# Opening of an attention layer: queries of the first head pair projected ahead of the second half of its keys

## The chip, the cores and the metric

One core of one Trainium2 chip. The metric is device microseconds (us) of one execution of the whole program. The engines are TensorE (PE, with its weight loads as PEld), VectorE (DVE), ScalarE (ACT), GpSimd (POOL) and SyncE (SP, which issues most DMAs). Each runs its own list of instructions in order and waits on semaphores for the others.

## What is computed

A decoder trunk of two layers over 1024 tokens of 1024 features. Layer 0 is a gated short convolution with a SwiGLU feed-forward network (FFN). Layer 1 is the attention this case is about, again with an FFN. Its core, cut from the reference:

```python
xn = _rms_norm(x, g[0])
shared = _shared_kv(x, kv_norm_g, kv_w)          # k, v = split(_rms_norm(h, g_kv) @ w_kv)
q = (x @ w_q).reshape(b, s, N_HEADS, HEAD_DIM) * (HEAD_DIM ** -0.5)
for (window, dil), (k_cat, v_cat) in zip(DILATED_GROUPS, shared):   # (128,1),(512,4),(2048,16)
    sc = einsum(q, k_cat) + bias                 # bias = -slope * distance, masked to the band
    p = exp(sc - max); den = sum(p); o = (p / den) @ v_cat
out = sum over the three, weighted by their softmax denominators
mix = out @ w_o
```

There are 16 heads of 64 features, worked in 8 pairs.

## The kernel before, in words

Products are done in about float32 accuracy: each operand is split into a high part (rounded to the matmul's type, by a CAST on ACT) and a low part (the rest, by a subtraction on DVE), and three products of 8 matmuls are summed (high by high, low by high, high by low). So a projection of 512 tokens for one head pair is 24 matmuls of 128x512 in one of two PSUM banks.

The **opening** stands between the last FFN product of layer 0 and the first attention step. In it the normalized tokens of the second half, tiles 4 to 7, are turned (transposed) by PE one by one, each by eight small matmuls out of `acc_tile`; ACT then makes `x_hi` (L1622) and DVE `x_lo` (L2252). Between these turns PE runs six projections for head pair 0 (`project_first`, L1538). They are named here K0, K1 (keys of tokens 0 to 511 and 512 to 1023), V0, V1 and Q0, Q1. The order is the table `OPENING`, of (part, half) with part 0 keys, 1 values, 2 queries. `TURNS` gives the matmul count ahead of which each of the four turns stands. A half-1 projection needs `x_lo` of all eight tiles.

The projection weights come as *chunks*: chunks 0, 1, 2 are the keys', values' and queries' weights of pair 0, chunks 3, 4, 5 those of pair 1. SP loads a chunk (`load_projection`) into one of two raw buffers, POOL multiplies it by the norm's gains (`scale_chunk`, L3426), and `prepare` makes its high part on ACT (L1611) and its low part on DVE (L2241). The split weights lie in three buffers: chunks 0 and 3 share `w_second_100`, 1 and 4 `w_second_98`, 2 and 5 `w_second_99`. So ACT's `prepare` of chunk 3 waits on `chunk_done`, which counts chunks whose half 1 is done:

```python
act.wait_ge(chunk_done.sem, moving + (min(n - SPLIT_RING + 1, chunk0["oproj"]) + CREDIT))
```

For chunk 3 that is one chunk of attention, the keys: K1 must have run. For chunk 4 it is V1.

A finished projection is taken by `project` on ACT (high part, L2088 keys, L2099 queries) and DVE (low part, L3012 keys, L3017 queries); values are turned by PE and split (L2105 ACT, L3027 DVE). The parts of keys and queries are then copied by DMAs on SP's queue into `k_stack` (all 1024 keys, four DMAs of 512 KB) and `q_stack` (four DMAs per half). The first scores matmul (L1555) waits for the stacked keys and for the first half of the stacked queries; `q_parts` holds one half at a time.

DVE also makes the **bias tables** in the opening: `distances` (L2985), `window_counts(0)` (L2970), `window_counts(1)` (L2973 to L2980, four operations), `window_counts(2)` (three), `masked_logs`, `log_of(2)`, `log_of(3)`, and `head_bias` (L3035, two operations). The bias is needed by DVE's first operation of an attention step, which adds it to the scores and finds the row's minimum (L3060). After that comes ACT's exponential (L2193), whose function table is loaded by an `ACT_TABLE_LOAD` ahead of it.

Of the kernel before, what the change touches and what calls it, by code (L numbers as in the profile page):

```python
# [21 lines left out]
F32 = mybir.dt.float32  # L22
# [8 lines left out]
HALF = 512  # L31
# [129 lines left out]
def trunk(nc, x, norm_g, conv_in_w, conv_w, conv_out_w, kv_norm_g, kv_w, q_w, o_w,  # L161
# [25 lines left out]
    with ExitStack() as ctx:  # L187
# [18 lines left out]
        rden = keep("rden", [2])  # L206
        neg_half = keep("neg_half", [1])


# [498 lines left out]

        OPENING = ((0, 0), (1, 0), (0, 1), (2, 0), (1, 1), (2, 1))
        TURNS = {22: HT, 36: HT + 1, 46: HT + 2, 48: HT + 3}  # L710

# [14 lines left out]
        def _(sp):  # L726
# [221 lines left out]
            def stack_first():  # L948
                for e in range(2):
                    sp.wait_ge(*k_lo_done.at("attn", 2))  # L950
                    for b in range(2):
                        sp.dma_start(att["k_stack"][b * HD:(b + 1) * HD, e].bitcast(F32),
                                     att["k_parts"][e * HD:(e + 1) * HD].bitcast(F32)).then_inc(k_stacked[e], 16)
                load_projection(5, 0)
                for h in range(2):
                    sp.wait_ge(*q_lo_done.at("attn", h + 1))
                    for e in range(2):
                        for b in range(2):
                            sp.dma_start(att["q_stack"][b * HD:(b + 1) * HD, e,
                                                        h * HALF:(h + 1) * HALF].bitcast(F32),  # L960
                                         att["q_parts"][e * HD:(e + 1) * HD, b].bitcast(F32)) \
                                .then_inc(q_stacked[e], 16)

            for pos in range(2, 5):
                load_projection(pos, 0)
            stack_first()
            with sp.Fori(0, PAIRS // 2 - 1) as g:
# [30 lines left out]
        def _(pe):  # L998
# [522 lines left out]
            def project_first(pos, i):  # L1521

                part, h = OPENING[pos]
                if i == 0:
                    if h == 0:
                        pe.wait_ge(*lo_ready.at("attn", part + 1))
                    if pos == 2:
                        pe.wait_ge(*xl_ready.at("norm2", TT))
                        pe.wait_ge(*k_lo_done.at("attn", 1))
                    elif pos == 3:  # L1530
                        pe.wait_ge(*v_done.at("attn", 1))
                    elif pos == 4:
                        pe.wait_ge(*k_lo_done.at("attn", 2))
                    elif pos == 5:
                        pe.wait_ge(*q_lo_done.at("attn", 1))
                n, k = i // KT, i % KT
                w, a = ((0, x_hi), (0, x_lo), (1, x_hi))[n]
                mm = pe.matmul(bank(PROJ + pos % 2),  # L1538
                               w_split(chunk0["attn"] + part)[:, w, k * P:(k + 1) * P],
                               a[:, k, h * HALF:(h + 1) * HALF],  # L1540
                               start=(i == 0), stop=(i == PER_HALF - 1))
                if i == PER_HALF - 1:
                    mm.then_inc((chunk_done if h else half_done).sem, 1)
# [28 lines left out]
        def _(act):  # L1572
# [417 lines left out]
            def down_layer(ph, norm_ph):  # L1990
# [69 lines left out]
                for i in range(HT + 2):  # L2060
                    if i < HT:
                        right_square(i)
                    if pre and i == HT + 1:
                        high_part(norm_ph, HT)
                    if pre and 0 <= i - 2 < HT:
                        second_square(norm_ph, HT + i - 2)
                if pre:
                    for t in range(HT + 1, TT - 1):
                        high_part(norm_ph, t)

# [125 lines left out]

            project((0, 0), 0, OPENING)
            high_part("norm2", TT - 1)
            prepare(chunk0["attn"] + 2)
            project((0, 0), 1, OPENING)  # L2200
            project((0, 0), 2, OPENING)
            prepare(chunk0["attn"] + 3)
            values_high((0, 0), 0, TURN)
            project((0, 0), 3, OPENING)
            project((0, 0), 4, OPENING)
            prepare(chunk0["attn"] + 4)
            values_high((0, 0), 1, TURN)
            project((0, 0), 5, OPENING)
            exponentials(0, 0)
# [16 lines left out]
        def _(dve):  # L2226
# [558 lines left out]
            def up_layer(ph, down):  # L2785
# [74 lines left out]
                for p in MIXED[1:3]:  # L2860
                    mix(ph, p, FT // 2 - 1)

            def down_layer(ph, norm_ph):

# [69 lines left out]
                for i in range(HT + 2):  # L2934
# [8 lines left out]
                    if pre and i >= 2 and i - 2 < HT - 2:  # L2943
                        normed(norm_ph, HT + i - 2)
                if pre:
                    normed(norm_ph, TT - 2)
                    low_part(norm_ph, HT)
                    normed(norm_ph, TT - 1)
                    for t in range(HT + 1, TT - 1):
                        low_part(norm_ph, t)  # L2950

# [49 lines left out]
            ins.then_inc(slope_ready.sem, 1)  # L3001

            def project(r, pos, order=ORDER):

                moving, fixed = r
                part, h = order[pos]
                b = PROJ + pos % 2
                cols = slice(h * HALF, (h + 1) * HALF)
                count = moving * 2 + (2 * fixed + h + 1)
                if part == 0:  # L3010
                    dve.wait_ge(*k_hi_done.at("attn", count))
                    dve.tensor_tensor(att["k_parts"][:, 1, cols], bank(b),  # L3012
                                      f32(att["k_parts"][:, 0, cols]), ALU.subtract) \
                       .then_inc(k_lo_done.sem, 1)
                elif part == 2:
                    dve.wait_ge(*q_hi_done.at("attn", count))
                    dve.scalar_tensor_tensor(out=att["q_parts"][:, 1], in0=bank(b),  # L3017
                                             scalar=-float(HD) ** -0.5,
                                             in1=f32(att["q_parts"][:, 0]),
                                             op0=ALU.mult, op1=ALU.subtract) \  # L3020
                       .then_inc(q_lo_done.sem, 1)

# [136 lines left out]

            project((0, 0), 0, OPENING)  # L3160
            low_part("norm2", TT - 1)
            prepare(chunk0["attn"] + 2)
            distances()
            window_counts(0)
            window_counts(1)
            project((0, 0), 2, OPENING)
            prepare(chunk0["attn"] + 3)
            values_low((0, 0), 0, TURN)
            window_counts(2)
            project((0, 0), 3, OPENING)  # L3170
            masked_logs()
            log_of(2)
# [19 lines left out]
        def _(pool):  # L3192
# [124 lines left out]
            def down_layer(ph, norm_ph):  # L3317
# [45 lines left out]
                for i in range(HT):  # L3363
                    gain_left(i)
                for i in range(HT + 2):
                    if i < HT:
# [84 lines left out]

            for c in (2, 3, 4):
                scale_chunk(c)
# [30 lines left out]
```

## Time and profile before

| what | before |
|---|---|
| time, median of 3 runs | 2276.36 us (2276.23 to 2277.83) |
| the profiled execution | 2276.5 us, its span 2274.7 us |
| PE busy | 2216.5 us, 97% of the span |
| DVE busy | 1688.2 us, 74% |
| ACT busy | 961.8 us, 42% |
| POOL busy | 485.3 us, 21% |
| opening | about 1010 to 1056 us of the span |

The span runs from the first to the last instruction; the program's own time has some 1.8 us more around it. All times of single instructions below are on the span's clock.

### The profile page before, as it was taken

Reading aid. Unit: us, or ns where it says so; the run is one execution under the profiler, and the core shown is the slowest. Engines: PE = TensorE matmul, PEld = TensorE weight load, DVE = VectorE, ACT = ScalarE, POOL = GpSimd, SP = SyncE. Lnnn points to the kernel's source line nnn. Section 1 sums busy time; section 2 is a strip of 40 time slices with the busy share of each in tenths; the row PEclk is TensorE's granted clock in tenths of the full one; section 3 lists DMA queues with packets and bytes.
Section 4 is the critical chain, followed back from the end, with each engine's and each line's share of the span. In section 5 each row is a group of like instructions: output and inputs, shape, how many; then the busy total and the mean of one; then the engine's idle time right before and its main releaser. Section 6 shows DMA issues by size and latency. Waiting matters only on the chain. (4 is left out here: it accounts for less than half of the span.)

```text
span 2274.7 us, 31865 instructions
## 1 busy us (share of the span) xinstructions
PE 2216.5 (97%) x10604; PEld 1849.1 (81%) x10604; DVE 1688.2 (74%) x2529; ACT 961.8 (42%) x1758; POOL 485.3 (21%) x416
## 2 busy tenths in 40 slices
PE   7999998999999999999999999999899999999998
PEld 6888787888888888877888888888788888888886
DVE  6988768777777667797767666676877777776768
ACT  4322255322222243564556656565532222223453
POOL 5000025333232101252110011002533333310113
PEclk9999999999999999999999999999999999999999
DMA  5122242333333487635333333234133333338764
GB/s 158 37 56 56 71 173 63 98 114 95 111 98 111 139 274 242 215 116 167 84 85 76 68 79 76 59 112 144 47 116 102 107 102 107 102 107 281 246 227 171
DMA packets 246010, 278.24 MB, mean 122 GB/s; under 512 B 18528, under 2 KB 157792, under 8 KB 243808
## 3 DMA queue, kind: packets, MB, share of 16 engines
q1 hardware_dynamic: 242656, 264.84, 38.0%
q10 hardware_dynamic: 3200, 11.54, 1.5%
q8 instruction: 74, 1.21, 0.2%
q14 instruction: 80, 0.66, 0.1%
HBM read 202.40 MB, written 48.76 MB: 110 GB/s over the span
## 5 line engine op out<-in xcount | busy, mean ns | idle before, releaser
L1249 PE MATMUL banks<-xb_mid,up_split 128*128 128x512 f32 x2064 | 475.8, 389 | 2.2 <-DVE up_split L2380 2.2
L1249 PEld LDWEIGHTS banks<-xb_mid,up_split 128*128 128x128 f32 x2064 | 387.1, 188 | 82.9 <-DVE up_split L2380 2.6
L1338 PE MATMUL banks<-down_split 128*128 128x512 f32 x1848 | 423.0, 390 | 4.5 <-DVE down_split L2747 3.2
L1338 PEld LDWEIGHTS banks<-down_split 128*128 128x128 f32 x1848 | 345.4, 188 | 80.7 <-DVE down_split L2747 7.8
L1249 PE MATMUL banks<-xb_low,up_split 128*128 128x512 f32 x1584 | 370.1, 392 | 4.3 <-issue 2.0
L1249 PEld LDWEIGHTS banks<-xb_low,up_split 128*128 128x128 f32 x1584 | 299.3, 189 | 67.7 <-DVE up_split L2380 3.1
L2747 DVE TENSOR_TENSOR down_split<-down_raw,down_split 128x1024 fp32r<-128x1024 f32 x154 | 199.3, 1294 | 107.2 <-ACT down_split L1954 106.9
L1954 ACT CAST down_split<-down_raw 128x1024 fp32r<-128x1024 f32 x154 | 162.0, 1052 | 203.9 <-PE banks L1338 166.2
L3389 POOL TENSOR_TENSOR sums<-raw_up 128x512 f32<-128x512 f32 x88 | 117.5, 1339 | 482.1 <-DMA raw_up<-in_ffn_in_w 261.9
L1383 PE MATMUL banks<-x_hi,w_second 128*128 128x512 f32 x672 | 176.3, 394 | 0.0
L3060 DVE CUSTOM_DVE_ANT_0 scores<-banks,bias 128x896 f32<-128x896 f32 (+7 forms) x128 | 96.7, 756 | 79.3 <-PE banks L1420 63.6
L2380 DVE TENSOR_TENSOR up_split<-raw_up,up_split 128x512 fp32r<-128x512 f32 x132 | 134.1, 1019 | 19.1 <-ACT up_split L1710 19.1
L1710 ACT CAST up_split<-sums 128x512 fp32r<-128x512 f32 x176 | 108.6, 617 | 86.9 <-PE banks L1249 84.0
L2380 DVE TENSOR_TENSOR up_split<-sums,up_split 128x512 fp32r<-128x512 f32 x176 | 126.1, 718 | 18.7 <-ACT up_split L1710 18.7
L1383 PEld LDWEIGHTS banks<-x_hi,w_second 128*128 128x128 f32 x672 | 120.5, 188 | 20.3
L3426 POOL TENSOR_TENSOR raw_second<-raw_second,gains 128x1024 f32<-128x1024 f32 x26 | 51.3, 1976 | 400.5 <-DMA raw_second<-in_q_w 186.4
L1986 ACT ACTIVATE gate<-gate 128x512 f32<-128x512 f32 x44 | 27.9, 634 | 243.1 <-DVE gate L2843 243.1
L2782 DVE TENSOR_TENSOR hid_mix<-hid 128x512 f32<-128x512 f32 x88 | 68.8, 782 | 76.0 <-DMA hid_spill<-hid_mix 76.0
L3075 DVE TENSOR_TENSOR pt<-banks,pt 128x896 fp32r<-128x896 f32 (+7 forms) x128 | 96.7, 756 | 29.4 <-ACT pt L2120 28.2
L2193 ACT ACTIVATE scores<-scores,neg_max 128x896 f32<-128x896 f32 (+7 forms) x128 | 100.7, 786 | 13.4 <-DVE neg_max L3060 13.1
L1710 ACT CAST up_split<-raw_up 128x512 fp32r<-128x512 f32 x132 | 81.0, 616 | 49.3 <-PE banks L1249 45.1
L1449 PE MATMUL banks<-pt,v_split 128*128 128x256 f32 x576 | 99.6, 299 | 0.1
(227 smaller groups left out, 3607.1 us busy)
## 6 DMA issues: line engine op xcount, KB each, us to landing
raw_up<-in_ffn_in_w SPq DMA_DIRECT2D x88, 512.0 KB, 5.0
down_raw<-in_ffn_out_w SPq DMA_DIRECT2D x154, 256.0 KB, 3.4
down_raw<-hid_spill SPq DMA_DIRECT2D x154, 256.0 KB, 4.1
hid_spill<-hid_mix SPq DMA_DIRECT2D x110, 256.0 KB, 4.8
down_second<-in_ffn_out_w SPq DMA_DIRECT2D x66, 256.0 KB, 3.3
k_stack<-k_parts SPq DMA_DIRECT2D x32, 512.0 KB, 6.3
hid_spill<-hid SPq DMA_DIRECT2D x44, 256.0 KB, 2.0
raw_up<-in_conv_in_w SPq DMA_DIRECT2D x18, 512.0 KB, 5.2
```

What stands on the lines that cost most here:

```text
L1249: mm = pe.matmul(bank(b_out), up_part(ph, p, a)[:, q * P:(q + 1) * P], block(RIGHT_OF[p], b)[:, q, :], start=(i == 0), stop=(i == len(pass ...
L1338: mm = pe.matmul(bank(b_out), side[:, a, 0, i * P:(i + 1) * P], side[:, b, 1, :], start=(p in (M3, M5, M1, M2) and first and j == 0), stop ...
L1383: mm = pe.matmul(bank(PROJ + pos % 2), w_split(chunk0["attn"] + c)[:, w, k * P:(k + 1) * P], a[:, k, h * HALF:(h + 1) * HALF], start=(i == ...
L1449: mm = pe.matmul(psum[:, OUT, 0:2 * P].rearrange("p (n q) -> p n q", n=2), att["v_split"][pair % 2][:, j, e, :], att["pt"][:, s % 2, :, j ...
L1710: act.copy(up_part(ph, p, 0), src).then_inc(up_hi.sem, 1)
L1954: act.copy(down_part(ph, q)[:, 0], down_raw[q % len(DOWN_AT)][:]) \
L2193: act.activation(att["scores"][:, s % 2, 0:n], att["scores"][:, s % 2, 0:n], ACT.Exp, bias=neg_max[:, s % 2:s % 2 + 1], scale=-1.0, accum_ ...
L2380: dve.tensor_tensor(up_part(ph, p, 1), src, f32(up_part(ph, p, 0)), ALU.subtract).then_inc(up_lo.sem, 1)
L2747: dve.tensor_tensor(down_part(ph, q)[:, 1], down_raw[q % len(DOWN_AT)][:], f32(down_part(ph, q)[:, 0]), ALU.subtract) \
L3060: dve.tensor_tensor_reduce(out=att["scores"][:, s % 2, 0:n], in0=psum_row(SCORE + apart(s, last), n), in1=att["bias"][:, SEQ - n:SEQ], sca ...
L3075: dve.tensor_tensor(att["pt"][:, s % 2, 1, 0:n], psum_row(PROB, n), f32(att["pt"][:, s % 2, 0, 0:n]), ALU.subtract) \
L3389: pool.tensor_tensor(weight_sum(out_), a, b, op).then_inc(summed.sem, 1)
```

## The change

It reorders the opening on all five engines; the work is the same but for one added exponential of a 128x1 tile. Q0 goes ahead of K1; the four turns are spread wider; POOL scales chunk 2 earlier and ACT and DVE split it earlier; SP stacks the first half of the queries ahead of its later loads; on DVE `window_counts(1)` goes behind the split of chunk 3; and ACT calls the exponential once on a scratch tile, so that its table is loaded ahead of the last query projection.

```diff
-        OPENING = ((0, 0), (1, 0), (0, 1), (2, 0), (1, 1), (2, 1))
-        TURNS = {22: HT, 36: HT + 1, 46: HT + 2, 48: HT + 3}
+        OPENING = ((0, 0), (1, 0), (2, 0), (0, 1), (1, 1), (2, 1))
+        TURNS = {28: HT, 40: HT + 1, 52: HT + 2, 62: HT + 3}
...
# PE, project_first
                     if pos == 2:
-                        pe.wait_ge(*xl_ready.at("norm2", TT))
                         pe.wait_ge(*k_lo_done.at("attn", 1))
                     elif pos == 3:
+                        pe.wait_ge(*xl_ready.at("norm2", TT))
                         pe.wait_ge(*v_done.at("attn", 1))
                     elif pos == 4:
+                        pe.wait_ge(*q_lo_done.at("attn", 1))
+                    elif pos == 5:
                         pe.wait_ge(*k_lo_done.at("attn", 2))
-                    elif pos == 5:
-                        pe.wait_ge(*q_lo_done.at("attn", 1))
...
# ACT, end of the last FFN product of layer 0
+                    if pre and i == HT:
+                        prepare(chunk0["attn"] + 2)
                     if pre and i == HT + 1:
                         high_part(norm_ph, HT)
...
# ACT, opening
             project((0, 0), 0, OPENING)
+            high_part("norm2", HT + 1)
+            high_part("norm2", HT + 2)
+            project((0, 0), 1, OPENING)
             high_part("norm2", TT - 1)
-            prepare(chunk0["attn"] + 2)
-            project((0, 0), 1, OPENING)
             project((0, 0), 2, OPENING)
             prepare(chunk0["attn"] + 3)
+            project((0, 0), 3, OPENING)
             values_high((0, 0), 0, TURN)
-            project((0, 0), 3, OPENING)
             project((0, 0), 4, OPENING)
             prepare(chunk0["attn"] + 4)
             values_high((0, 0), 1, TURN)
+            act.activation(table_junk[:], neg_half[:], ACT.Exp)
             project((0, 0), 5, OPENING)
...
# DVE, end of the last FFN product of layer 0
                 if pre:
+                    project((0, 0), 0, OPENING)
+                    prepare(chunk0["attn"] + 2)
                     normed(norm_ph, TT - 2)
                     low_part(norm_ph, HT)
                     normed(norm_ph, TT - 1)
-                    for t in range(HT + 1, TT - 1):
-                        low_part(norm_ph, t)
+                    low_part(norm_ph, HT + 1)
...
# DVE, opening
-            project((0, 0), 0, OPENING)
+            low_part("norm2", HT + 2)
             low_part("norm2", TT - 1)
-            prepare(chunk0["attn"] + 2)
             distances()
             window_counts(0)
-            window_counts(1)
             project((0, 0), 2, OPENING)
             prepare(chunk0["attn"] + 3)
-            values_low((0, 0), 0, TURN)
+            window_counts(1)
             window_counts(2)
             project((0, 0), 3, OPENING)
+            values_low((0, 0), 0, TURN)
             masked_logs()
...
# POOL: chunk 2 scaled between gain_left and whole_root of the last FFN product
+                if pre:
+                    scale_chunk(2)
...
-            for c in (2, 3, 4):
+            for c in (3, 4):
                 scale_chunk(c)
```

On DVE the place is the opening. `dist_i`, `dist`, `bias`, `scores` and `neg_log` are the tables' names (`scores` is scratch here), `w_second_100` is the buffer of chunks 0 and 3. Before:

```order
L2985 CAST dist<-dist_i 128x1024
L2970 TENSOR_SCALAR scores<-dist 128x1024
L2973 TENSOR_SCALAR bias<-dist_i 128x1024
L2975 TENSOR_SCALAR scores<-bias 128x1024
L2977 SCALAR_TENSOR_TENSOR scores<-dist,scores 128x1024
L2980 TENSOR_TENSOR scores<-scores 128x1024
L3012 TENSOR_TENSOR k_parts<-banks,k_parts 128x512
L2241 TENSOR_TENSOR w_second_100<-raw_second,w_second_100 128x1024
L3027 TENSOR_TENSOR v_split_122<-banks,v_split_122 128x8x64
L2973 TENSOR_SCALAR bias<-dist_i 128x1024
L2975 TENSOR_SCALAR scores<-bias 128x1024
L2980 TENSOR_TENSOR scores<-scores 128x1024
```

and with the change:

```order
L2997 TENSOR_SCALAR scores<-dist 128x1024
L2883 SCALAR_TENSOR_TENSOR q_parts<-banks,q_parts 128x512
L2247 TENSOR_TENSOR w_second_100<-raw_second,w_second_100 128x1024
L3000 TENSOR_SCALAR bias<-dist_i 128x1024
L3002 TENSOR_SCALAR scores<-bias 128x1024
L3004 SCALAR_TENSOR_TENSOR scores<-dist,scores 128x1024
L3007 TENSOR_TENSOR scores<-scores 128x1024
L3000 TENSOR_SCALAR bias<-dist_i 128x1024
L3002 TENSOR_SCALAR scores<-bias 128x1024
L3007 TENSOR_TENSOR scores<-scores 128x1024
L2878 TENSOR_TENSOR k_parts<-banks,k_parts 128x512
L3034 TENSOR_TENSOR v_split_122<-banks,v_split_122 128x8x64
```

The low part of K1 (`k_parts`) stood behind the first of two counts and ahead of chunk 3's split; now it stands behind that split and both counts.

On ACT the place is the same stretch, with the semaphores that each row waits for. Before:

```order
L2088 CAST k_parts<-banks 128x512 [waits chunk_done]
L1611 CAST w_second_100<-raw_second 128x1024 [waits chunk_done,w_scaled]
L2105 CAST v_split_122<-banks 128x8x64 [waits v_turned]
L2099 ACTIVATE q_parts<-banks 128x512 [waits half_done]
L2093 COPY v_t<-banks 128x512 [waits v_turned,chunk_done]
```

and with the change:

```order
L2103 ACTIVATE q_parts<-banks 128x512 [waits half_done]
L1616 CAST w_second_100<-raw_second 128x1024 [waits chunk_done,w_scaled]
L2092 CAST k_parts<-banks 128x512 [waits chunk_done]
L2109 CAST v_split_122<-banks 128x8x64 [waits v_turned]
L2097 COPY v_t<-banks 128x512 [waits v_turned,chunk_done]
```

Q0 is taken first, and the split of chunk 3 now stands ahead of K1's high part instead of behind it; both wait for K1.

On SP's queue, from the third chunk's load on. Before:

```order
L739 DMA raw_second<-in_q_w 128x8x128 [waits lo_ready]
L739 DMA raw_second<-in_kv_w 128x8x128 [waits lo_ready] x2
L952 DMA k_stack<-k_parts 64x2048 [waits k_lo_done]
L952 DMA k_stack<-k_parts 64x2048
L952 DMA k_stack<-k_parts 64x2048 [waits k_lo_done]
L952 DMA k_stack<-k_parts 64x2048
L739 DMA raw_second<-in_q_w 128x8x128 [waits lo_ready]
L959 DMA q_stack<-q_parts 64x512 [waits q_lo_done]
```

and with the change:

```order
L740 DMA raw_second<-in_kv_w 128x8x128 [waits lo_ready]
L961 DMA q_stack<-q_parts 64x512 [waits q_lo_done]
L961 DMA q_stack<-q_parts 64x512 x3
L740 DMA raw_second<-in_kv_w 128x8x128 [waits lo_ready]
L740 DMA raw_second<-in_q_w 128x8x128 [waits lo_ready]
L953 DMA k_stack<-k_parts 64x2048 [waits k_lo_done]
L953 DMA k_stack<-k_parts 64x2048
L953 DMA k_stack<-k_parts 64x2048 [waits k_lo_done]
L953 DMA k_stack<-k_parts 64x2048
L961 DMA q_stack<-q_parts 64x512 [waits q_lo_done]
```

The first four query copies moved ahead of the loads of chunks 4 and 5, and the key copies stand behind both loads.

## Rows read from the trace of the kernel before

**Rows 1.** Instructions of L1538, PE: duration ns min/median/max, first and last start us.

```profile
L1538 PE MATMUL banks<-x_hi,w_second x96: 387/389/504, 1010.5 to 1051.8; 128*128 128x512 f32 x96
```

**Rows 2.** Timeline of PE, opening: start us, us, instruction, [idle before <-releaser].

```profile
1016.64 1.09 PE L1058 MATMUL banks<-ident,acc_tile 128*128 128x128 f32 x8 [0.97 <-DVE acc_tile L2367]
...
1029.11 2.14 PE L1538 MATMUL banks<-x_hi,w_second 128*128 128x512 f32 x8 [2.36 <-DVE x_lo L2252]
...
1032.91 3.80 PE L1538 MATMUL banks<-x_hi,w_second 128*128 128x512 f32 x16
...
1053.82 0.44 PE L1555 MATMUL banks<-k_stack,q_stack 128*128 128x128 f32 x2 [1.66 <-DMA q_stack<-q_parts]
...
1056.18 0.50 PE L1420 MATMUL banks<-k_stack,q_stack 128*128 128x256 f32 x2 [0.51 <-DVE neg_max L3060]
1056.98 0.33 PE L1435 MATMUL banks<-ident,scores 128*128 128x128 f32 x1 [0.30 <-ACT scores L2193]
```

**Rows 3.** Timeline of DVE, opening, from `window_counts(1)` to the first bias addition.

```profile
1031.55 0.69 DVE L2973 TENSOR_SCALAR bias<-dist_i 128x1024 int32<-128x1024 int32 x1
...
1035.61 0.69 DVE L3012 TENSOR_TENSOR k_parts<-banks,k_parts 128x512 fp32r<-128x512 f32 x1
1036.49 1.23 DVE L2241 TENSOR_TENSOR w_second<-raw_second,w_second 128x1024 fp32r<-128x1024 f32 x1 [0.18 <-ACT w_second L1611]
...
1039.86 2.80 DVE L2980 TENSOR_TENSOR scores<-scores 128x1024 f32<-128x1024 f32 x1
...
1047.93 1.22 DVE L2241 TENSOR_TENSOR w_second<-raw_second,w_second 128x1024 fp32r<-128x1024 f32 x1 [0.70 <-ACT w_second L1611]
...
1051.77 3.17 DVE L3035 SCALAR_TENSOR_TENSOR bias<-dist,slope,neg_log 128x512 f32<-128x512 f16 x2
1055.23 0.69 DVE L3017 SCALAR_TENSOR_TENSOR q_parts<-banks,q_parts 128x512 fp32r<-128x512 f32 x1 [0.30 <-ACT q_parts L2099]
1055.84 0.28 DVE L3060 CUSTOM_DVE_ANT_0 scores<-banks,bias 128x128 f32<-128x128 f32 x1
```

**Rows 4.** Timeline of ACT, opening.

```profile
1020.80 1.06 ACT L1683 ACTIVATE junk<-resid 128x1024 bf16<-128x1024 f32 x1 [0.34 <-DVE resid L2353]
...
1035.41 1.05 ACT L1611 CAST w_second<-raw_second 128x1024 fp32r<-128x1024 f32 x1
...
1054.53 0.60 ACT L2099 ACTIVATE q_parts<-banks 128x512 fp32r<-128x512 f32 x1 [5.38 <-DMA q_stack<-q_parts]
1055.14 1.28 ACT L2193 ACT_TABLE_LOAD   x1
1056.43 0.40 ACT L2193 ACTIVATE scores<-scores,neg_max 128x128 f32<-128x128 f32 x1
```

**Rows 5.** Timeline of POOL, opening.

```profile
1008.17 0.26 POOL L3342 TENSOR_SCALAR mean<-square,mean 128x1 f32<-128x1 f32 x1 [11.25 <-ACT junk L1683]
...
1022.87 0.99 POOL L3445 IOTA dist_i<- 128x1024 int32 x1
...
1039.60 1.98 POOL L3426 TENSOR_TENSOR raw_second<-raw_second,gains 128x1024 f32<-128x1024 f32 x1 [11.58 <-DMA raw_second<-in_kv_w]
1051.70 1.90 POOL L3426 TENSOR_TENSOR raw_second<-raw_second,gains 128x1024 f32<-128x1024 f32 x1 [10.12 <-DMA raw_second<-in_q_w]
```

**Rows 6.** Timeline of SP: the issue of chunk 2's load.

```profile
1000.90 0.38 SPq L739 DMA_DIRECT2D raw_second<-in_q_w  x1
```

**Rows 7.** DMA issues of 999 to 1004 us: KB each, median us to landing.

```profile
raw_second<-in_q_w SPq DMA_DIRECT2D x1, 512.0 KB, 3.9
```

**Rows 8.** DMA issues of 960 to 1062 us.

```profile
k_stack<-k_parts SPq DMA_DIRECT2D x4, 512.0 KB, 8.4
```

**Rows 9.** Groups of DVE instructions, 1020.7 to 1056 us: busy us, mean ns, idle before.

```profile
L2252 DVE TENSOR_TENSOR x_lo<-banks,x_hi 128x1024 fp32r<-128x1024 f32 x4 | 4.9, 1216 | 0.5 <-ACT x_hi L1622 0.5
```

**Rows 10.** Stretches: start:end, length, busy us of PE, PEld, DVE, ACT, POOL, PEclk, DMA share, GB/s.

```profile
262.80:266.20 3.40, 0.23 (x2) 0.04 (x1) 3.14 (x5) 1.59 (x3) 0.00 (x0) 1.00 0.35 115
266.20:269.60 3.40, 3.40 (x8) 2.73 (x9) 3.40 (x6) 0.49 (x1) 0.00 (x0) 0.50 0.39 149
```

More of the change, by code:

```diff
@@ L207, in trunk @@
         neg_half = keep("neg_half", [1])
+        table_junk = keep("table_junk", [1])
         KB = 1024
@@ L953, in stack_first, with queries_first @@
                                      att["k_parts"][e * HD:(e + 1) * HD].bitcast(F32)).then_inc(k_stacked[e], 16)
[L954 to L964, printed above, removed]
+                queries_first(1)
+            def queries_first(h):
+                sp.wait_ge(*q_lo_done.at("attn", h + 1))
+                for e in range(2):
+                    for b in range(2):
+                        sp.dma_start(att["q_stack"][b * HD:(b + 1) * HD, e,
+                                                    h * HALF:(h + 1) * HALF].bitcast(F32),
+                                     att["q_parts"][e * HD:(e + 1) * HD, b].bitcast(F32)) \
+                            .then_inc(q_stacked[e], 16)
+            for pos in range(2, 4):
                 load_projection(pos, 0)
+            queries_first(0)
+            load_projection(4, 0)
+            load_projection(5, 0)
             stack_first()
@@ L2066, in down_layer @@
                         second_square(norm_ph, HT + i - 2)
-                if pre:
-                    for t in range(HT + 1, TT - 1):
-                        high_part(norm_ph, t)
             up_layer("up0", "norm1", "down0")
@@ L2861, in up_layer, with project @@
                     mix(ph, p, FT // 2 - 1)
+            def project(r, pos, order=ORDER):
+                moving, fixed = r
+                part, h = order[pos]
+                b = PROJ + pos % 2
+                cols = slice(h * HALF, (h + 1) * HALF)
+                count = moving * 2 + (2 * fixed + h + 1)
+                if part == 0:
+                    dve.wait_ge(*k_hi_done.at("attn", count))
+                    dve.tensor_tensor(att["k_parts"][:, 1, cols], bank(b),
+                                      f32(att["k_parts"][:, 0, cols]), ALU.subtract) \
+                       .then_inc(k_lo_done.sem, 1)
+                elif part == 2:
+                    dve.wait_ge(*q_hi_done.at("attn", count))
+                    dve.scalar_tensor_tensor(out=att["q_parts"][:, 1], in0=bank(b),
+                                             scalar=-float(HD) ** -0.5,
+                                             in1=f32(att["q_parts"][:, 0]),
+                                             op0=ALU.mult, op1=ALU.subtract) \
+                       .then_inc(q_lo_done.sem, 1)
             def down_layer(ph, norm_ph):
@@ L2948, in down_layer @@
                     normed(norm_ph, TT - 1)
-                    for t in range(HT + 1, TT - 1):
-                        low_part(norm_ph, t)
+                    low_part(norm_ph, HT + 1)
             up_layer("up0", "down0")
@@ L3001, in _ @@
             ins.then_inc(slope_ready.sem, 1)
[L3003 to L3021, printed above, removed]
             def values_low(r, h, b=PROJ + 1):
```

## The prediction

> **What bounds the kernel now.** I read PE first, since it is busy nearly all the time: what it loses in the opening moves the end of the program. Its projections run from 1010.5 to 1051.8 us [rows 1]; sixteen matmuls take 3.80 us [rows 2], the last of them 0.389 [rows 1], so one starts every (3.80 - 0.389) / 15 = 0.227 us. Next the waits in PE's timeline: 0.97 us for tile 4's normalized tokens, 2.36 for the last low part of x (K1 needs all of them), 1.66 for the DMA that stacks Q0, 0.51 and 0.30 in the first attention step [rows 2]. Together 5.8 us. They are what a better order of PE could win.
>
> Then I asked who stands behind the last of these waits, because that decides what a gain upstream is worth. DVE's first bias addition stands at 1055.84 [rows 3]. Between 1031.55 and 1055.84, 24.3 us, DVE was idle 0.18, 0.70 and 0.30 us, no more [rows 3]. The last idle time waits for ACT's Q1, and ACT had waited 5.38 us for the stacking of Q0 [rows 4]. So at the end of the opening the DMA is last, but by 0.30 us alone: DVE, full of table work, is nearly tied with it. Taking away PE's and the DMA's waits gives 0.3 us as long as DVE does not get done sooner; making DVE later costs in full. So the question is what the change does to DVE.
>
> One thing inflates DVE's time. The table operation at 1039.86 took 2.80 us; POOL's scaling of chunk 4 ran from 1039.60 to 1041.58 [rows 3, 5]. The two `head_bias` operations at 1051.77 took 3.17; POOL's scaling of chunk 5 ran from 1051.70 to 1053.60. In both cases DVE ends about 1.1 to 1.3 us after POOL does, as if it had begun there: it lost 1.7 and 1.8 us, 3.5 in all.
>
> **The change part by part.**
>
> *POOL's earlier scaling.* It takes 1.9 to 2.0 us [rows 5]. Chunk 2's load is issued at 1000.9 [rows 6] and lands 3.9 us later [rows 7], so POOL can do it from 1004.8 to 1006.8, inside the 11.25 us of idle time before 1008.17. Cost nothing; without that cover it would delay the whole norm by up to 2.0.
>
> *The end of the FFN on DVE and ACT.* DVE now takes K0's low part and splits chunk 2 ahead of the last two tiles. But K0's high part stands on ACT behind the square that began at 1020.80 and takes 1.06 [rows 4], so it is there at 1021.9 + 0.6 = 1022.5 (0.6: as for Q1 in rows 4). DVE's low part ends at 1023.1. POOL's iota runs from 1022.87 for 0.99 [rows 5], and the split of chunk 2, which like the table operations reads and writes SBUF only, would begin when that ends: 1023.9 to 1025.0 (1.2 a split, rows 3).
>
> *PE up to K1.* The four turns are a turn's eight transposes of about 0.85 us each (1.09 with the drain of the last, rows 2). Tile 4's turn, now at matmul 28, comes at 1010.5 + 28 x 0.227 = 1016.9, after its tokens (1016.64 before): the 0.97 is won. PE is at Q0 at 1010.5 + 48 x 0.227 + 1.7 = 1023.1 and waits for chunk 2's split until 1025.0: 1.9 lost in place of the 2.36. The third turn then waits for DVE's low part of tile 4 (1025.0 + 0.7 + 1.2 [rows 9] = 1026.9; PE is there at 1025.9): 1.0 more, perhaps 0.2 at the last one. So K1 ends at T = 1010.5 + 96 x 0.227 + 4 x 0.85 + 0.4 (turn of the values) + about 3.0 = 1039.1. With no wait at all it would be 1036.1; if POOL's scaling of chunk 3 gets in before DVE's last normalizations, 1.9 later, 1041.
>
> *The hold on DVE.* This is the term that decides. DVE reaches the split of chunk 3 early: the last turn ends near 1030.8, ACT's part takes 1.0 and DVE's 1.2 [rows 9], so the last low part of x ends near 1033.2 (DVE waits for it); two table operations and Q0's low part follow, 2.0 us, so 1035.2. There it waits for ACT's high part, which overwrites the keys' weights and so waits for K1, until T + 1.1 (ACT's cast is 1.05, rows 4) = 1040.2: 5 us idle. Before, the same split came behind K1's low part and cost 0.18 of waiting [rows 3]. Behind it now stand, in DVE's queue, both window counts, then K1's low part, then everything up to the first bias addition. That is the work that DVE did from 1031.55 to 1055.84, without the Q0 low part, which is done: 24.3 - 0.18 - 0.70 - 0.30 - 0.6 = 22.5 us, with POOL's two collisions in it. They stay: chunk 4's load now stands behind Q0's stacking on SP, so it is issued after 1035.2 and lands, at 3.9 us, not before 1039.1, and more likely near 1041.6 with four issues ahead of it; chunk 5's load waits for chunk 3's split at 1041.4 and lands at 1045.3. Both scalings then meet DVE in its counts. So the first bias addition comes at 1040.2 + 22.5 = 1062.7 instead of 1055.84: 6.9 us later.
>
> *Who waits for that.* V1 runs on until T + 5.5 = 1044.6, but Q1 needs the bank that K1's low part frees. That low part ends after the split (1.2), the counts (4.0 for the first, about 2.7 for the second) and 3.5 of collisions: 1040.2 + 12.1 = 1052.3. So PE waits some 7.7 us at Q1. Q1 then ends at 1058 and ACT and DVE can take it in time. The key copies are issued at 1052.4 and land 8.4 us later at the worst price before [rows 8], 1060.8, ahead of 1062.7. So neither is last; DVE is.
>
> *The early table.* The exponential waited for its load: 1.28 us from 1055.14, the exponential at 1056.43 [rows 4], while DVE's minimum was done at 1055.84 + 0.28 = 1056.1. Loading early gives 0.3, which is also PE's wait in rows 2. The bounds are 0 (it is hidden by PE's filling matmuls) and 0.5. The load itself falls into ACT's idle time before Q1. The Trainium skill, "ScalarE: Activation LUTs", section "What ACT_TABLE_LOAD costs", gives 1283 ns for the load, which this trace agrees with, and 1380 ns of drain, 2.66 us a switch; the exponential here starts 0.01 us after the load's end, so the trace shows no drain behind it. By the page's price up to 1.7 us would come back and the sum would be +5.2 in place of +6.6.
>
> *SP.* Q0's stacking moves ahead of two loads, so Q1 can overwrite `q_parts` without the 5.38 us wait; with DVE late that is worth nothing.
>
> Sum: +6.9 - 0.3 = +6.6 us on the profiled execution of 2276.5, which is 0.1 above the median: 2283.0 us, +0.29%. From there on the steps are as before: PE is nearly full and nothing gives the time back.
>
> **The rivals.**
>
> *Same: the hold is there but costs less.* T may be as early as 1036.1 (3.0 less), and one collision or both may fall into DVE's idle time before 1040.2 (1.7 or 3.5 less). All of it would leave +0.1, and any 2.0 of it bring the sum under the 4.6 us that are 0.2% (about what a measurement of this kernel can tell from no change). Against it: POOL got in first in both cases of rows 5, and the loads can hardly land earlier.
>
> *Same: no hold.* If ACT's count were reached without K1, DVE would go on at 1035.2 + 1.2 + 21.3 = 1057.7, +1.6 with the table. The code's count is the keys' chunk, so this needs a misreading of mine.
>
> *Slower still.* After long idle time PE's clock has fallen: before 266.2 us PE did 0.23 us of work in 3.4, and the next 3.4 us ran at a granted clock of 0.50, 1.2 GHz [rows 10], eight matmuls in the time of fifteen, some 1.6 us lost. After the 7.7 us wait Q1 would end at 1060, still ahead of DVE. But a second fall before the first scores would be on the path: +8.2, and with T at 1041 +10.
>
> *Faster: PE and the DMA are the bound, not DVE.* If the first attention step starts when PE and the stacks are ready, the 5.8 us of rows 2 come back: 2270.7. It speaks for it that PE's last wait names the DMA. It decides at K1's low part: it would have to be out by about 1041, that is, the split of chunk 3 and the counts would have to be done before K1 ends. DVE's rows with the change have them in between, and an engine works its list in order.
>
> **How the numbers follow.** Forecast (+4.6 to +8): 0.56. Slower still (+8 to +10): 0.13. Hold at less cost (0 to +4.6): 0.20. No hold: 0.05. Faster: 0.06. So slower by over 0.2% 0.69, within 0.2% 0.25, faster 0.06. The range leaves out the faster case, the cheapest tenth and the dearest few: 2278.0 (+1.6) to 2286.0 (+9.6).
>
> **What the changed profile would show.** DVE idle some 5 us ahead of a `w_second` split, ended by ACT; PE idle 7 to 8 us ahead of its last projection, ended by DVE's `k_parts`; the first L3060-like operation near 1062.7; POOL's two scalings beside stretched count operations; the table load in ACT's idle time; the waits of 0.97 and 1.66 gone. I am wrong if K1's low part ends before 1048, or if the first bias addition comes before 1059 although the hold is there: then the collisions or T were mis-sized. If both are as said and the time is not, something behind the opening gives it back.

## The result and the profile after

The changed kernel takes 2286.58 us (median of 6 runs, 2286.06 to 2288.4), the kernel before in the same session 2276.84 (6 runs): ratio 1.0042 [1.0033, 1.0052], some 9.7 us slower. The forecast was 2283.0, with a range up to 2286.0. The sign and the mechanism were right; one term of the sum was 3.1 us too small. The profiled execution took 2286.39 us (span 2284.6).

The opening of the changed kernel, PE first (start us, duration us, instruction, idle time before it and what ended it). These rows answer to [rows 1, 2]; the opening begins at 1010.90 here, 0.38 later than before, and all differences below are taken from that start.

```profile
L1543 PE MATMUL banks<-x_hi,w_second x96: 387/389/792, 1010.9 to 1062.7; 128*128 128x512 f32 x96
```

```profile
1024.71 1.21 PE L1543 MATMUL banks<-x_hi,w_second 128*128 128x512 f32 x4 [0.95 <-DVE w_second L2247]
1028.24 1.94 PE L1063 MATMUL banks<-ident,acc_tile 128*128 128x128 f32 x8 [2.32 <-DVE x_lo L2258]
1029.83 1.85 PE L1543 MATMUL banks<-x_hi,w_second 128*128 128x512 f32 x4
...
1055.42 3.57 PE L1543 MATMUL banks<-x_hi,w_second 128*128 128x512 f32 x8 [7.46 <-DVE k_parts L2878]
...
1063.21 0.41 PE L1560 MATMUL banks<-k_stack,q_stack 128*128 128x128 f32 x2
...
1066.09 0.50 PE L1425 MATMUL banks<-k_stack,q_stack 128*128 128x256 f32 x2 [1.02 <-DVE neg_max L3067]
```

The wait for the stacked queries is gone: the first scores (L1560) start without one. In its place PE waits 7.46 us at Q1 for K1's low part. The last projection matmul starts at 1062.7 instead of 1051.8. DVE, which answers to [rows 3]:

```profile
1023.44 1.22 DVE L2247 TENSOR_TENSOR w_second<-raw_second,w_second 128x1024 fp32r<-128x1024 f32 x1
1024.58 2.39 DVE L2373 TENSOR_SCALAR acc_tile<-resid,rstd 128x1024 f32<-128x1024 f32 x1
...
1037.62 0.69 DVE L2883 SCALAR_TENSOR_TENSOR q_parts<-banks,q_parts 128x512 fp32r<-128x512 f32 x1
1043.70 1.23 DVE L2247 TENSOR_TENSOR w_second<-raw_second,w_second 128x1024 fp32r<-128x1024 f32 x1 [5.39 <-ACT w_second L1616]
1044.84 0.69 DVE L3000 TENSOR_SCALAR bias<-dist_i 128x1024 int32<-128x1024 int32 x1
1045.56 2.27 DVE L3002 TENSOR_SCALAR scores<-bias 128x1024 f32<-128x1024 int32 x1
...
1050.38 2.27 DVE L3000 TENSOR_SCALAR bias<-dist_i 128x1024 int32<-128x1024 int32 x1
...
1054.67 0.69 DVE L2878 TENSOR_TENSOR k_parts<-banks,k_parts 128x512 fp32r<-128x512 f32 x1
...
1065.75 0.28 DVE L3067 CUSTOM_DVE_ANT_0 scores<-banks,bias 128x128 f32<-128x128 f32 x1
```

The hold stands where it was forecast, 5.39 us ahead of the split of chunk 3, ended by ACT. Behind it DVE does not rest until the first bias addition, 22.05 us later. ACT and POOL, which answer to [rows 4, 5]:

```profile
1042.62 1.05 ACT L1616 CAST w_second<-raw_second 128x1024 fp32r<-128x1024 f32 x1 [5.72 <-PE banks L1543]
...
1060.07 1.28 ACT L2213 ACT_TABLE_LOAD   x1
1061.37 0.20 ACT L2213 ACTIVATE table_junk<-neg_half 128x1 f32<-128x1 f32 x1
...
1066.07 0.41 ACT L2197 ACTIVATE scores<-scores,neg_max 128x128 f32<-128x128 f32 x1 [2.33 <-DVE neg_max L3067]
```

```profile
1005.44 1.90 POOL L3434 TENSOR_TENSOR raw_second<-raw_second,gains 128x1024 f32<-128x1024 f32 x1 [8.12 <-DMA raw_second<-in_q_w]
...
1023.20 0.99 POOL L3453 IOTA dist_i<- 128x1024 int32 x1
1024.16 2.25 POOL L3434 TENSOR_TENSOR raw_second<-raw_second,gains 128x1024 f32<-128x1024 f32 x1
1045.04 2.24 POOL L3434 TENSOR_TENSOR raw_second<-raw_second,gains 128x1024 f32<-128x1024 f32 x1 [18.63 <-DMA raw_second<-in_kv_w]
1049.14 2.96 POOL L3434 TENSOR_TENSOR raw_second<-raw_second,gains 128x1024 f32<-128x1024 f32 x1 [1.86 <-DMA raw_second<-in_q_w]
```

ACT's cast at 1042.62 waits for PE's matmuls: K1 ended just ahead of it. Each of POOL's last three scalings has one stretched DVE operation beside it (2.39, 2.27 and 2.27 us). Three stretches of the same execution show PE's clock (start:end, length, busy us and count of PE, PEld, DVE, ACT, POOL, granted clock, DMA share, GB/s):

```profile
1024.50:1027.90 3.40, 1.21 (x4) 0.67 (x4) 3.40 (x3) 0.00 (x0) 1.91 (x1) 1.00 1.01 407
1027.90:1031.30 3.40, 3.06 (x12) 2.80 (x13) 2.04 (x6) 1.08 (x2) 0.00 (x0) 0.50 1.03 414
...
1055.20:1058.60 3.40, 3.18 (x8) 2.50 (x9) 3.30 (x6) 0.00 (x0) 0.00 (x0) 0.50 0.72 142
```

The clock fell to 0.50, 1.2 GHz, twice: behind the waits of 0.95 and 2.32 us on the way to K1, where eight transposes took 1.94 us and four matmuls 1.85, and behind the 7.46 us wait at Q1.

**Where the time went.** The first bias addition stands 54.85 us behind the opening's start (1065.75 - 1010.90), before it was 45.32 (1055.84 - 1010.52): 9.53 us. The exponential follows it by 0.32 us instead of 0.59, which gives back 0.27. That makes 9.26 of the 9.9 us between the profiled executions; 0.38 lies ahead of the opening, and the last 0.3 I can't assign.

### The profile page after: what moved, and what is told of

Read it like the earlier page. It is cut to its first block and busy times, and to the rows that moved or that the text cites. A ratio compares the mean times of both kernels' runs of the same rounds, so it can differ in the third digit from the quotient of the medians.

```text
span 2284.6 us, 31866 instructions
## 1 busy us (share of the span) xinstructions
PE 2221.4 (97%) x10604; PEld 1852.7 (81%) x10604; DVE 1689.6 (74%) x2529; ACT 962.1 (42%) x1759; POOL 486.7 (21%) x416
```

## Experiments

All were timed beside the kernel before, whose medians lay between 2276.49 and 2276.91. "Opening" below is the time from the first projection matmul to the first bias addition, 45.32 us before and 54.85 with the change. The start itself varies between profiled executions by 1.7 us (1009.20 to 1010.93), also where the code ahead of it is the same (1010.90 with the change, 1009.31 in experiment 1), so differences are taken within an execution.

**1. The hold taken away.** The changed kernel with `prepare(3)` behind K1 on ACT and DVE:

```diff
# DVE (ACT alike)
             project((0, 0), 2, OPENING)
-            prepare(chunk0["attn"] + 3)
             window_counts(1)
             window_counts(2)
             project((0, 0), 3, OPENING)
+            prepare(chunk0["attn"] + 3)
             values_low((0, 0), 0, TURN)
```

> The changed kernel, with chunk 3's split on ACT and DVE moved behind K1's taking, and both window counts ahead of it; all else as changed. Hold theory (DVE waits 5.4 us for K1 at chunk 3's split with 6.8 us of counts queued behind it): the wait of 5.4 us goes, PE's 7.5 us wait for K1's low part goes, the first bias addition comes about 5 us earlier (near 1060.5 instead of 1065.8), time 2281.5 us, 5 us under the changed kernel and still 4 to 5 over the one before, since K1 itself ends 7 us later than before and POOL's two scalings still collide. Rival, late K1 alone (the loss is that K1 ends 7 us later, and DVE's order does not matter): within 1 us of the changed kernel's 2286.6.

2282.46 us (7 runs), ratio 1.0024 [1.0013, 1.0036]; the opening took 50.46 us. The hold and PE's wait at Q1 are gone, and 4.1 us came back of the 9.7. But a new wait stands ahead of the first scores:

```profile
1058.59 0.66 PE L1560 MATMUL banks<-k_stack,q_stack 128*128 128x128 f32 x2 [4.95 <-DMA k_stack<-k_parts]
```

```profile
1047.75 0.37 SPq L740 DMA_DIRECT2D raw_second<-in_q_w  x1
1048.17 5.79 SPq L953 DMA_DIRECT2D k_stack<-k_parts  x4
```

K1's low part was out at 1045.3, but SP held the four copies of the keys behind chunk 5's load, which waited for the split of chunk 3. The hold has passed from DVE's queue to SP's. It was not yet what set the first bias addition: DVE worked without a pause from the last low part of x to that addition at 1059.77, so its list was the bound. That the gain stayed under the expected 5 us has another cause. In this execution PE's clock stayed low for longer on the way to K1 (four and six matmuls took 2.06 and 2.71 us, with the change 1.85 and 1.55), and the last low part of x began 25.46 us after the opening's start instead of 24.13. Behind the wait of 4.95 us the clock was low again (2.87 us for six matmuls, against 1.62 with the change):

```profile
1028.25 2.06 PE L1543 MATMUL banks<-x_hi,w_second 128*128 128x512 f32 x4
1030.10 2.71 PE L1543 MATMUL banks<-x_lo,w_second 128*128 128x512 f32 x6
...
1059.04 2.87 PE L1388 MATMUL banks<-x_hi,w_second 128*128 128x512 f32 x6
```

```profile
1034.77 1.23 DVE L2258 TENSOR_TENSOR x_lo<-banks,x_hi 128x1024 fp32r<-128x1024 f32 x1 [3.86 <-ACT x_hi L1627]
```

**2. POOL kept out of the normalizations.** The changed kernel with one wait on POOL:

```diff
+            pool.wait_ge(*xn_ready.at("norm2", HT))
             for c in (3, 4):
                 scale_chunk(c)
```

> The changed kernel, with POOL made to wait for DVE's last normalization before it scales chunk 3. Theory: POOL's scaling got in ahead of DVE's normalization of tile 6 and held it 1.7 us, which made PE wait 2.3 us at tile 6's turn, and the 3.4 us behind that wait ran at a granted clock of 0.50. Without it the normalization takes 0.7 us, the turn's wait is 0.6, K1 ends 1.7 us earlier, 3 us if the half clock goes too; time 2284.9 or 2283.5 us. Rival: K1's end is not on the path, since DVE is late anyway: within 0.5 us of 2286.6.

2282.63 us (8 runs), ratio 1.0026 [1.0016, 1.0037]: 4.0 us came back, more than I expected. The opening took 51.91 us, 2.94 less than with the change; the excess over that is within the interval. DVE's normalization of tile 6, PE's two waits and ACT's cast of chunk 3:

```profile
1024.35 0.75 DVE L2373 TENSOR_SCALAR acc_tile<-resid,rstd 128x1024 f32<-128x1024 f32 x1
...
1040.40 1.23 DVE L2247 TENSOR_TENSOR w_second<-raw_second,w_second 128x1024 fp32r<-128x1024 f32 x1 [5.41 <-ACT w_second L1616]
```

```profile
1024.49 1.20 PE L1543 MATMUL banks<-x_hi,w_second 128*128 128x512 f32 x4 [0.96 <-DVE w_second L2247]
1026.38 1.06 PE L1063 MATMUL banks<-ident,acc_tile 128*128 128x128 f32 x8 [0.69 <-DVE x_lo L2258]
1027.20 1.17 PE L1543 MATMUL banks<-x_hi,w_second 128*128 128x512 f32 x4
```

```profile
1039.32 1.05 ACT L1616 CAST w_second<-raw_second 128x1024 fp32r<-128x1024 f32 x1 [5.77 <-PE banks L1543]
```

The normalization takes 0.75 us instead of 2.39, the wait at the turn of tile 6 falls from 2.32 to 0.69, and the transposes and matmuls behind it run at full clock (1.06 and 1.17 us). So the cast, and K1's end just ahead of it, come 28.65 us after the opening's start instead of 31.72. The hold itself stays (5.41).

**3. The early table alone.** The kernel before with the early exponential of the diff.

> The kernel before, with the early exponential alone. Theory: the table load was on the path by 0.3 us only: 2276.5 us, 0.3 under the kernel before, no more than the measurement tells. Rival by the page's price of a switch, with a drain behind the load: 1.7 us less, 2275.1.

2276.62 us (11 runs), ratio 1.0003 [0.9994, 1.0012]: the exponential follows the bias addition by 0.32 us instead of 0.59, and the total cannot tell it. In this execution the stacking of Q0 also landed sooner, and PE's wait for it fell from 1.66 to 0.90 us. DVE then took Q1's low part without the 0.30 us of idle time before it:

```profile
1053.38 0.44 PE L1556 MATMUL banks<-k_stack,q_stack 128*128 128x128 f32 x2 [0.90 <-DMA q_stack<-q_parts]
```

```profile
1055.15 0.69 DVE L3019 SCALAR_TENSOR_TENSOR q_parts<-banks,q_parts 128x512 fp32r<-128x512 f32 x1
```

PE's first scores came 0.74 us sooner after the opening's start, the first bias addition only 0.38 (44.94 us): DVE was last by then.

**4. The queries stacked earlier.** The kernel before with the early exponential, and on SP the first half of Q0's stacking ahead of chunk 5's load.

```diff
-                load_projection(5, 0)
                 for h in range(2):
+                    if h == 1:
+                        load_projection(5, 0)
                     sp.wait_ge(*q_lo_done.at("attn", h + 1))
```

> The kernel before, in its own order, with the early exponential and with SP stacking Q0 ahead of chunk 5's load instead of behind it. Theory: before, the last wait of the opening was for Q0's stacking (landed at 1053.8, 0.5 MB of weights ahead of it in the queue), tied with DVE, which had lost 1.8 us to POOL's scaling of chunk 5 in the last table operations. With the load behind, the stacking lands near 1051.5 and POOL scales chunk 5 after the first bias addition, so that both bounds fall: first bias addition near 1053.7 instead of 1055.8, and 0.3 for the table; time 2274.4 us, 2.4 under the kernel before. Rival: PE's queue or the key stack is next at once: 2276.5, the table's 0.3 alone.

2274.98 us (11 runs), ratio 0.9994 [0.9985, 1.0003]; PE's first scores no longer wait for the DMA, and POOL scales chunk 5 only at 1053.63, behind the table work. Yet the opening of this execution is only 0.31 us shorter (45.01), where I had expected about 2. The reason is PE's clock. Ahead of K1 PE waited 2.36 us, as in the kernel before, but here the clock fell behind that wait:

```profile
1027.81 2.73 PE L1540 MATMUL banks<-x_hi,w_second 128*128 128x512 f32 x8 [2.36 <-DVE x_lo L2255]
1030.34 3.01 PE L1540 MATMUL banks<-x_lo,w_second 128*128 128x512 f32 x8
```

The same sixteen matmuls took 2.14 and 1.99 us in the kernel before. ACT took K1 25.99 us after the opening's start instead of 24.40, so 1.6 us were lost there. What the earlier stacking is worth at the same clock this trace does not show.

**5. Both mends.** Experiments 1 and 2 together.

> The changed kernel with both mends: ACT and DVE split chunk 3 behind K1's taking (both window counts ahead of it), and POOL scales chunk 3 only behind DVE's last normalization. My theory (an early or late K1 matters in either order, since K1's end sets chunk 3's split, chunk 5's load behind it and the keys' stacking behind that): the two gains of 4.1 and 3.95 us add up, no long idle time on DVE, K1 taken some 3 us earlier than in the first, first bias addition near 1057, 2278.3 us. Rival (K1's end mattered only through DVE's hold; without the hold DVE's list of table work is the bound): 2281 to 2282.5, hardly below the first mend alone.

2278.43 us (11 runs), ratio 1.0005 [0.9996, 1.0014]; opening 45.94 us. The gains add up (8.2 us of 9.7). But it is not K1's end that matters here, as I had expected: DVE did not wait for K1. The last low part of x, which follows PE's turn of tile 7, began 21.05 us after the opening's start instead of 25.46 in experiment 1. From there DVE worked without a pause for 24.9 us (25.0 in experiment 1) to the first bias addition. SP's queue still holds the keys back, and chunk 5's scaling still meets DVE's table work (2.20 us at 1051.06):

```profile
1055.45 0.66 PE L1560 MATMUL banks<-k_stack,q_stack 128*128 128x128 f32 x2 [4.75 <-DMA k_stack<-k_parts]
```

```profile
1031.85 1.22 DVE L2258 TENSOR_TENSOR x_lo<-banks,x_hi 128x1024 fp32r<-128x1024 f32 x1 [1.96 <-ACT x_hi L1627]
...
1051.06 2.20 DVE L3022 TENSOR_SCALAR scores<-scores 128x1024 f32<-128x1024 f32 x1
```

**6. The keys' stacking ahead of chunk 5's load**, on top of both mends.

```diff
             load_projection(4, 0)
-            load_projection(5, 0)
             stack_first()
...
# stack_first, behind the copies of the keys
+                load_projection(5, 0)
                 queries_first(1)
```

> The kernel with both mends, and on SP's queue the four copies that stack the keys ahead of the load of chunk 5 (which waits for chunk 3's split) instead of behind it. If PE's wait for the stacked keys was set by that place in the queue: the wait of some 5 us ahead of the first scores is gone or passes to DVE, chunk 5's scaling on POOL moves out of DVE's table work, 2275.5 to 2277.5 us. Rival (the copies themselves are slow, or DVE is done no sooner): the same time as with both mends alone, 2278 us, with PE waiting for the DMA or for DVE's bias.

2277.12 us (11 runs), ratio 0.9999 [0.9990, 1.0009]; opening 44.32 us. The opening is 1.62 us shorter than in experiment 5, most of it because chunk 5's load, now behind the keys, brings POOL's scaling only at 1056.55: the table operation that took 2.20 us takes 0.68. PE no longer waits for a DMA. It waits for DVE instead, and the next stretch runs at half clock:

```profile
1050.66 0.33 PE L1560 MATMUL banks<-k_stack,q_stack 128*128 128x128 f32 x2
...
1055.60 0.50 PE L1425 MATMUL banks<-k_stack,q_stack 128*128 128x256 f32 x2 [3.18 <-DVE neg_max L3067]
```

```profile
1051.09 0.68 DVE L3022 TENSOR_SCALAR scores<-scores 128x1024 f32<-128x1024 f32 x1
```

```profile
1056.20:1059.60 3.40, 3.40 (x9) 2.72 (x10) 0.79 (x4) 0.76 (x3) 1.90 (x1) 0.50 0.43 98
```

**7. One collision taken away.** The changed kernel, POOL waiting for the first row minimum ahead of chunk 5's scaling.

```diff
                 scale_chunk(c)
+            pool.wait_ge(*max_done.at("attn", 1))
             with pool.Fori(0, PAIRS // 2 - 1) as g:
```

> The changed kernel; POOL waits for the first row minimum of attention before it scales chunk 5, so that this scaling no longer meets DVE's table work. My theory (DVE's chain behind the split of chunk 3 sets the end, and a table operation that meets a scaling waits for it): the operation that took 2.27 us beside the scaling at 1049.14 takes 0.69, first bias addition 1.6 us earlier, 2285.0 us. Rival (PE, through Q1 and the keys' stacking, is last and DVE is slack): no change, 2286.6. Rival (the scaling then meets the first attention steps and costs the same there): no change either, but with the operation at 0.69 us.

2283.92 us (8 runs), ratio 1.0030 [1.0019, 1.0040]. The opening took 53.17 us, 1.68 less than with the change, as expected; the operation took 0.69 instead of 2.27. The median gained 2.7; the excess over 1.7 is about what the interval leaves open.

**8. Less work on DVE.** The changed kernel without `window_counts(2)`.

> The changed kernel without the third window's count (its three table operations on DVE are left out, so keys of that window do not count in the bias). My theory (DVE's chain sets the end): those operations stand from 1050.38 to 1054.67, 4.3 us with one collision of 1.6 in it that may move to the next operation; so 2.7 to 4.3 us come back, 2282.3 to 2283.9 us, and PE's wait at Q1 falls from 7.5 to about 3.5 us. Rival (PE, the late K1 and its low clock set the end): the bias is done sooner, but the time stays near 2286.6.

2283.22 us (11 runs), ratio 1.0024 [1.0015, 1.0033]. The opening took 52.01 us, 2.84 less, and PE's wait at Q1 fell to 4.78. DVE work behind the hold is on the path almost one to one: the three operations span 4.3 us, and the collision of 1.6 moved to the next operation (2.84 us instead of 1.23).

**9. DVE relieved.** Experiment 6, with `distances` and `window_counts(0)` ahead of the last low part of x, and on DVE the split of chunk 4 behind the first row minimum.

```diff
# DVE
-            low_part("norm2", TT - 1)
             distances()
             window_counts(0)
+            low_part("norm2", TT - 1)
...
-            prepare(chunk0["attn"] + 4)
             values_low((0, 0), 1, TURN)
...
# DVE, attend, behind invert(s)
+                    if s0 == 0 and s == 0:
+                        prepare(chunk0["attn"] + 4)
```

> The kernel with both mends and the keys stacked ahead of chunk 5's load, and on DVE the first two table operations ahead of the low part of x of tile 7 (for which DVE idled 1.96 us) and the split of chunk 4 behind the first row minimum instead of ahead of the first bias (1.22 us). My theory: there PE already has its scores at 1050.7, and waits 3.18 us for DVE, whose list is the bound; so 1.4 + 1.2 = 2.6 us come back, PE's wait falls to about 0.6 us, 2274.5 us, 2 us under the kernel before. Rival (what DVE gets done sooner is lost later, by the moved split within the first attention steps, or PE's clock falls anyway): 2276 to 2277 us.

2273.51 us (11 runs), ratio 0.9984 [0.9975, 0.9994]: the one version measurably faster than both kernels. Opening 42.56 us; PE's wait fell to 1.34, and no stretch of the opening or of the first attention steps has the low clock. Against experiment 6 the opening is 1.76 us shorter, of the 2.6 expected; another 1.6 us is clock, since the nine matmuls behind PE's wait took 0.71 and 1.77 us instead of 1.20 and 2.84. The two moves on DVE were not tried apart.

```profile
1050.37 0.33 PE L1560 MATMUL banks<-k_stack,q_stack 128*128 128x128 f32 x2
...
1053.46 0.50 PE L1425 MATMUL banks<-k_stack,q_stack 128*128 128x256 f32 x2 [1.34 <-DVE neg_max L3067]
```

**10. The control**: experiment 4 (old order) with DVE's split of chunk 4 moved as in 9.

> Control: the kernel before with the early exponential and its queries stacked ahead of chunk 5's load, and the split of chunk 4 on DVE behind the first row minimum. In the old order PE comes to its scores only at 1052.3 to 1054.6 and then waits 0.5 us for DVE, so by my theory DVE's relief is worth at most 0.5 us here: 2274.5 to 2275 us. Rival (DVE is the bound in the old order as well): 1.2 us, 2273.8 us.

2274.72 us (11 runs), ratio 0.9991 [0.9982, 1.0000]; opening 45.04 us, against 45.01 without the move. DVE is done sooner and only waits longer for PE's turned values:

```profile
1049.47 0.69 DVE L3030 TENSOR_TENSOR v_split<-banks,v_split 128x512 fp32r<-128x512 f32 x1 [2.42 <-ACT v_split L2107]
```

So in the old order, as these two executions have it, PE is the bound once the queries are stacked early, and DVE has slack. With the new order and the mends PE is at its first scores 39.8 us after the opening's start (1050.37 - 1010.56), in the old order 43.1 (1052.26 - 1009.20). Of these 3.3 us some 1.6 are clock: here too, as in experiment 4, it fell behind the 2.36 us wait ahead of K1 (ACT took K1 at 25.97 us), and in experiment 9 it did not fall. That leaves some 1.7 us for the new order itself, an estimate. The medians of experiments 9 and 10 differ by 1.2 us, and their intervals overlap.

## Why the prediction came out as it did

**The bound** was right: PE's last wait before named a DMA, but DVE's list was nearly tied with it. In experiment 3, where the stacking landed sooner, DVE ended last and let 0.38 of the 0.74 us through. Experiment 4, which took the DMA's wait away, can't tell, since PE's clock fell in it. With the change DVE is the bound: experiment 8 took work off DVE behind the hold and it came back. Measured against the same operations unstretched, each of POOL's two collisions before cost 1.6 us (1.23 us at 1034.27, and 1.54 with the change), not 1.7 and 1.8.

**The hold** was right in place and size: 5.39 us against 5, and the chain behind it 22.05 us against 22.5, with both collisions in it. PE's wait at Q1 was 7.46 against 7.7. Experiment 1 shows the hold as a cause; only 4.1 us came back there, and in the profiled execution PE's clock cost 1.3 us more ahead of the last low part of x.

**T, the end of K1, is the step that failed.** The forecast had it 28.6 us after the opening's start (1039.1 - 1010.5); ACT's cast behind it came at 31.72, 3.1 later. With that, 6.9 + 3.1 - 0.45 (the shorter chain) gives 9.55 us; the first bias addition lost 9.53. Two things were mis-sized. POOL's scaling of chunk 3 got in ahead of DVE's normalization of tile 6. I had this as the dearer end of T, priced at 1.9, and not as the likeliest case. It happened in all four profiled executions without the wait on POOL (with the change and in experiments 1, 7 and 8: 2.39 us each time). It stretched PE's wait by 1.63 us (2.32 against 0.69 in experiment 2). And PE's clock fell behind this wait, which I had considered only behind the long one at Q1: 0.88 us on eight transposes and 0.68 on four matmuls. Together 3.2; experiment 2 took both away by one wait on POOL and brought the cast to 28.65.

It is partly by luck that the forecast's 28.6 is also the value without the collision. I had charged 1.9 us at Q0, because chunk 2's split was to wait for POOL's iota. It did not: it took 1.22 us beside the iota (1023.20 to 1024.19), and PE waited 0.95. In experiment 2 the two waits together were 1.65 us where the sum had about 3.0, and some 1.3 us of PE's own time was missing from the sum: two errors that cancelled. The Trainium skill, "SBUF — State Buffer", section "Who interferes with whom", says that a DVE instruction with two SBUF inputs contends with a GpSimd instruction that reads SBUF, not with one that only writes it. Of DVE's 2-port modes, which a `tensor_scalar` can enter, it says that whoever issues first gets the shared ports for the whole instruction. The trace agrees on both counts: the split, with two SBUF inputs, passed the iota unhindered, and the normalization, a TENSOR_SCALAR, came at 1024.58, after the scaling had begun at 1024.16, and took 2.39 us instead of 0.75. I had put the collision's delay on the wrong pair of instructions.

**POOL's earlier scaling** was free, as said (1005.44, in idle time). **The table** gave 0.27 against 0.3; the exponential of the early load started 0.02 us behind it (1061.37), so no row shows the drain that would have returned 1.7.

**The clock behind the Q1 wait** fell as the rival said, and cost nothing: Q1 was done when DVE was not. The "faster" rival needed K1's low part by 1041; experiment 9 has it there (1040.73, 0.69 long) and is the one that is faster. Experiments 5 and 6 had it begin at 1041.73 and 1041.85 and were not faster, so this alone does not decide.

## What to carry to other kernels

When a prepared operand's split waits for another engine to release a buffer, look at what stands behind that split in every in-order queue it passes, on DVE and on the queue that issues the DMAs: the same late event held both here, and curing one showed the other. When PE's order is improved and the time gets worse, look at the engine that ends last in that stage; a few small reorderings on ACT, POOL, SP and DVE turned +9.7 us into -3.4. If one engine's instruction can slip in ahead of another's at a point with no wait between them, price that as the likely case, and ask whether the wait it makes on PE is enough to cost clock as well.

## What the runs showed of the hardware

Waits much shorter than the 7.46 us at Q1 lowered PE's clock as well: 0.95 and 2.32 us, with four matmuls between them, were followed by a stretch at 0.50, and so was the 3.18 us wait in experiment 6; behind 0.96 and 0.69 us (experiment 2) and behind 1.34 us (experiment 9) it stayed at full. The length of a wait alone did not decide it. Behind the 2.36 us ahead of K1 in the old order the clock stayed at 1.00 in two executions (the kernel before and experiment 3) and fell in two others (experiments 4 and 10: 0.69 and 0.70 in the next 3.4 us, 1.6 us lost); why, no run here shows. The 7.46 us wait cost PE clock and yet no time, because DVE was later still. And in the changed kernel a DVE operation that met a POOL scaling lost 1.6 us for a scaling of 2.2 to 3.0, while the iota beside the split cost it nothing.
